# Three edits to the order of waits in a two-layer hybrid diffusion backbone: landing semaphores per row, later column sums, earlier query copies

## The reference

```python
for i in range(2):
    sh, sc, g = split(silu(c) @ ada_w[i] + ada_b[i], 3)      # modulation, for latent and for context
    u = rmsnorm(h, norm_g[i]) * (1 + sc) + sh
    if i == 0:   # window attention with a sink (8 heads) beside a Hyena long convolution (1024 wide)
        a, b = window_attention(q, k, v), hyena(u)            # q, k, v, hyena inputs, gate = u @ ev_w_in
        o = concat([a, b]) * silu(gate)
    else:        # grouped-query attention with rope (8 heads) beside latent attention (8 heads)
        o = concat([gqa(q, k, v), mla(q_up, kv_up)]) * silu(gate)   # latent tokens only
    h = h + g * (o @ w_out[i])
return h_lat
```

## Time and profile before

| | |
|---|---|
| three runs | 1456.12, 1457.83, 1458.51 us (median 1457.83) |
| profiled execution | 1455.26 us, span 1453.4 us, mean granted clock of TensorE 0.991 |
| busy share of the span | PE 97%, PEld (weight loads) 78%, DVE 72%, ACT 39%, POOL 24% |
| DMA | 273.28 MB, mean 188 GB/s |
| chain that ended last | PE 81%, DVE 9%, DMA 4%, ACT 2%, issue 2% |

### The profile page before, as it was taken

The page is one execution under the profiler, slowest core; times in us unless marked ns, Lnnn a source line. Parts: engine busy times, 40 slices in busy tenths (PEclk is TensorE's granted clock), DMA queues, the critical chain, the costliest instruction groups (busy, mean ns, idle before and its releaser), DMA issues.

```text
span 1453.4 us, 18246 instructions
## 1 busy us (share of the span) xinstructions
PE 1404.1 (97%) x7208; PEld 1134.6 (78%) x7208; DVE 1039.9 (72%) x1246; ACT 566.6 (39%) x826; POOL 354.5 (24%) x333
## 2 busy tenths in 40 slices
PE   5999999999999999998999899999999999999998
PEld 1336888888888878877888688888988878899887
DVE  3384999999999878887888545555645677677554
ACT  2554222222222344433433312214436666666432
POOL 1000543334433021201120133442100135432000
PEclk9999999999999999999999999999999999999999
DMA  9998555564555554445456866651424342323674
GB/s 348 406 371 330 175 174 200 159 208 157 201 162 166 189 180 148 151 154 192 140 185 231 300 204 221 220 189 63 159 87 151 139 145 91 114 94 110 224 239 145
DMA packets 63221, 273.28 MB, mean 188 GB/s; under 512 B 6736, under 2 KB 13088, under 8 KB 43296
## 3 DMA queue, kind: packets, MB, share of 16 engines
q1 hardware_dynamic: 42960, 194.51, 38.1%
q0 software_dynamic: 20176, 77.61, 16.7%
HBM read 257.40 MB, written 14.69 MB: 187 GB/s over the span
## 4 chain that ended last, share of the span: by engine, by line
PE 81%; DVE 9%; DMA 4%; ACT 2%; issue 2%; SPq 1%; POOL 0%; DVEq 0%; ACTq 0%
PE banks L1068 16%; PE banks L1069 16%; PE banks L1072 16%; DMA ada_ring<-in_ada_first 2%; PE banks L2268 2%; PE banks L2269 2%; PE banks L2274 2%; PE banks L1274 2%; DVE wl L1030 2%; PE banks L2025 2%; PE banks L2022 2%; PE banks L2019 2%; PE banks L2293 2%; PE banks L582 1%; DVE ada_acc L417 1%
## 5 line engine op out<-in xcount | busy, mean ns | idle before, releaser
L1068 PE MATMUL banks<-xh,wh 128*128 128x512 f32 (+1 forms) x1296 | 473.4, 373 | 0.0
L1069 PE MATMUL banks<-xl,wh 128*128 128x512 f32 (+1 forms) x1296 | 468.5, 369 | 0.0
L1030 DVE TENSOR_TENSOR wl<-raw,wh 128x2048 fp32r<-128x2048 f32 (+1 forms) x125 | 284.2, 2274 | 104.3 <-ACT wh L1024 104.3
L1024 ACT ACTIVATE wh<-raw 128x2048 fp32r<-128x2048 f32 (+1 forms) x125 | 236.7, 1894 | 241.0 <-PE banks L1072 126.5
L1068 PEld LDWEIGHTS banks<-xh,wh 128*128 128x128 f32 x1296 | 245.0, 189 | 46.4 <-issue 5.7
L1072 PE MATMUL banks<-xh,wl 128*128 128x512 f32 (+1 forms) x1296 | 279.8, 368 | 0.3 <-DVE wl L1030 0.3
L1069 PEld LDWEIGHTS banks<-xl,wh 128*128 128x128 f32 x1296 | 245.1, 189 | 40.3 <-issue 0.2
L1072 PEld LDWEIGHTS banks<-xh,wl 128*128 128x128 f32 x1296 | 227.1, 189 | 41.0 <-DVE wl L1030 0.5
L440 POOL DMA_DIRECT2D ada_w<-in_ada_rest x128 | 69.8, 545 | 486.4 <-DVE ada_acc L429 317.7
L417 DVE SCALAR_TENSOR_TENSOR ada_acc<-ada_w,cond,ada_acc 128x1024 f32<-128x1024 f32 x120 | 166.9, 1391 | 4.8 <-DMA ada_w<-in_ada_rest 2.8
L429 DVE SCALAR_TENSOR_TENSOR ada_acc<-ada_w,cond,ada_acc 128x1024 f32<-128x1024 f32 x90 | 131.4, 1460 | 0.0
(11 more groups left out here) (387 smaller groups left out, 2125.7 us busy)
## 6 DMA issues: line engine op xcount, KB each, us to landing
ada_w<-in_ada_rest POOLq DMA_DIRECT2D x128, 512.0 KB, 4.1
raw<-in_ev_tiles SPq DMA_DIRECT2D x52, 1024.0 KB, 6.5
ada_ring<-in_ada_first SPq DMA_DIRECT2D x32, 1024.0 KB, 12.9
raw<-in_out_tiles SPq DMA_DIRECT2D x16, 1024.0 KB, 6.2
raw<-in_od_wide SPq DMA_DIRECT2D x16, 1024.0 KB, 4.9
raw<-in_od_gates SPq DMA_DIRECT2D x16, 1024.0 KB, 5.0
raw<-in_out_wide SPq DMA_DIRECT2D x16, 1024.0 KB, 5.8
hT<-in_hT POOLq DMA_DIRECT2D x4, 1024.0 KB, 11.9
```

The costliest lines, as they stand in the source:

```text
L1024: nc.scalar.activation(b.wh[:, t % 2, 0:width], b.raw[:, t % 2, 0:width], ACT.Copy).then_inc(s.hi_done, 1)
L1030: nc.vector.tensor_tensor(b.wl[:, t % 2, 0:width], b.raw[:, t % 2, 0:width], b.wh[:, t % 2, 0:width].bitcast(F32), ALU.subtract).then_inc( ...
L1068: nc.tensor.matmul(out, wh[:, k, :], b.xh[:, seg, k, :], start=(k == 0), stop=False)
L1069: nc.tensor.matmul(out, wh[:, k, :], b.xl[:, seg, k, :], start=False, stop=False)
```

## The change

Three edits, independent of one another. First, `O_LAND` and `O_LANDED` go: rows whose buffer is one of the first seven use the semaphore of that buffer, the five rows of the other buffers (rows 6 to 10) use the five landing semaphores of the start's modulation ring (renamed `ring_landed`), counted on from there. A row waits for its own landing, or for the second landing in its buffer. With it the load of output tile 1's weights goes from between rows 11 and 12 to behind row 15. Second, the last three `ADA_SLOTS` are one higher, for TensorE's column sums and VectorE's store alike. Third, in layer 1 ScalarE copies the turned queries ahead of the slot's weight cut. The renaming in the start block is left out here.

```diff
-O_LAND = (0, 1, 2, 3, 4, 5, 6, 0, 1, 2, 3, 4, 0, 1, 2, 3)
-O_LANDED = (2, 2, 2, 2, 2, 1, 1, 2, 2, 2, 2, 2, 3, 3, 3, 3)
 O_ORDER = (0, 1, 2, 3, 4, 5, 6, 8, 9, 10, 11, 12, 13, 14, 7, 15)
 O_SLOT = (0, 1, 2, 3, 4, 5, 7, 8, 9, 10, 11, 6, 0, 1, 2, 3)
...
-ADA_SLOTS = (9, 17, 25, 33, 41, 49)
+ADA_SLOTS = (9, 17, 25, 34, 42, 50)
...
-                if i == 33:
+                if i == 34:
                     pe.wait_ge(s.rs_step, 2)
-                if i == 41:
+                if i == 42:
                     pe.wait_ge(s.rs_step, 5)
                 ada_columns(nc, pe, b, s, ps[7], n)
...
+def o_landed(s, n):
+    slot = O_SLOT[n]
+    if slot < ORING:
+        return s.out_o_in[slot], 16 * O_SLOT[:n + 1].count(slot)
+    i = slot - ORING
+    return s.ring_landed[i], 16 * (len(range(i, ADA_PIECES, ADA_RING)) + 1)
...
-    sp.dma_start(b.orow[O_SLOT[n]][:], g.o_d[k]).then_inc(s.out_o_in[O_LAND[n]], 16)
+    sp.dma_start(b.orow[O_SLOT[n]][:], g.o_d[k]).then_inc(o_landed(s, n)[0], 16)
...
-    act.wait_ge(s.out_o_in[O_LAND[n]], 16 * O_LANDED[n])
+    act.wait_ge(*o_landed(s, n))
...
         for n in range(11, KT):
-            if n == 12:
-                load_raw(sp, b, s, t0 + 1, out_weights(g, 1), (KT, P))
             load_o(sp, b, s, g, n)
+        load_raw(sp, b, s, t0 + 1, out_weights(g, 1), (KT, P))
...
         for i in range(4, L1_TILES):
             if i == FIRST_GATE:
                 token_drains(*DRAIN_SLOT[i])
+            if i - 1 in QUERY_TURN:
+                for r in range(2):
+                    keep_queries(QUERY_TURN[i - 1], r, 4 + r, 2 * (i - 20) + r + 1)
             split_high(nc, act, b, s, t0 + i + 1, l1_width(i + 1))
...
-            if i - 1 in QUERY_TURN:
-                for r in range(2):
-                    keep_queries(QUERY_TURN[i - 1], r, 4 + r, 2 * (i - 20) + r + 1)
```

More of the change, by code:

```diff
@@ L527, in _ @@
             sp.dma_start(b.ada_ring[p % ADA_RING], g.ada_first[p].rearrange("p (h k n) -> p h k n", h=2, k=2)).then_inc(
-                s.ada_pe_landed[p % ADA_RING], 16)
+                s.ring_landed[p % ADA_RING], 16)
             if p == 2:
@@ L577, in ada_matmuls @@
             grp, r = divmod(p, 4)
-            pe.wait_ge(s.ada_pe_landed[p % ADA_RING], 16 * (p // ADA_RING + 1))
+            pe.wait_ge(s.ring_landed[p % ADA_RING], 16 * (p // ADA_RING + 1))
             if r == 0 and grp > 0:
@@ L2889, in semaphores @@
     s.ada_lat = sem("ada_lat")
-    s.ada_pe_landed = [sem(f"ada_pe_landed{i}") for i in range(ADA_RING)]
+    s.ring_landed = [sem(f"ring_landed{i}") for i in range(ADA_RING)]
     s.ada_pe_used = sem("ada_pe_used")
```

## The result

The changed kernel takes 1446.51 us in the median of six runs (1444.86 to 1449.3), the kernel before 1458.83 in six runs beside them: a ratio of 0.9918, with a 95% interval from 0.9905 to 0.9931 (below, a ratio is given with its interval in brackets). The forecast was 1443.8, its range 1441 to 1449.

A forecast was written before the change was run, and what follows sets the result against it. TensorE was taken to bound the kernel, so only its waits and slowed stretches pay; -7.1 - 7.4 + 0.5 = -14.0 us, from a median of 1457.83 to 1443.8, range 1441 to 1449.

The forecast's parts named there:

- Part 1: Column sums one slot later: at slot 41, 4.8 us of wait and 2.3 of slow tile go; -7.1 us.
- rival (b): VectorE takes the column-sum gain back, TensorE waiting for low weights in slots 42 to 51: -6.9 us, 1450.9; chance 0.07.
- Part 2: Landing semaphore per row, output tile 1's weights behind row 15: output tile 1 starts at 821.3, not 828.69; -7.4 us.
- They do: In output tile 0, rows keep up with TensorE: they land 0.68 us apart, row 11 lands 2.7 us after issue.
- Rival (a): The clock drops in front of output tile 1 after 2.5 us idle, costing 2.3 us: -11.7, 1446.1; chance 0.2.
- Part 3: Layer 1, turned queries copied ahead of the weight cut: 2.2 us wait shrinks, later waits for weights appear; +0.5 us.
- Rival (c): Layer 1's query move keeps the 2.2 us it removes, VectorE's delay being absorbed: -16.7 us in all, 1441.1; chance 0.12.
- (d): Gated rows don't come earlier, another event holding ScalarE; the row change is worth -0.6: -7.2 us, 1450.6; chance 0.04.
- (e): Slower: output tile 1's weights starve, deciding point 17.8 us after issue; at 21 us, 3.2 slower, 1461.0; chance 0.03.

The follow-up runs named there:

- the hold: Changed kernel with GpSimd's first two 0.5 MB loads held until all 16 gated rows are cut; 1445.22 us, ratio 0.9914; again 1445.29 us, 0.9909.
- the second execution with both: Changed kernel, output tile 1's weights behind the eleven early rows, rope turns behind row 15, query copies in old place; second execution 1442.52 us, ratio 0.9893.

## Why the prediction came near, and where it was wrong

**Part 1** was right: -7.1 forecast, -7.12 in the trace, -7.4 in the run of its own. Tile 41 takes 7.36 us (655.62 to 662.98) at clock 1.00, so the 2.3 us of half clock came back together with the 4.8 us of waiting. No wait for low weights follows in slots 42 to 51; rival (b) is out.

**Part 2** was right in what it removes and wrong in one step: "They do", of rows that keep up, with row 11 landing 2.7 us and the weights 6.1 us after their issue. Both times came from a stretch in which GpSimd's loads were already through. The prediction never placed these two loads on the new scale. Counted from the first attention product behind tile 51, row 11's issue moved from +7.26 to +2.84, while the loads moved the other way, from +0.97 to +2.72, since GpSimd's work on the rope turns ahead of them took 6.56 us (795.21 to 801.77) instead of 4.74 (803.23 to 807.97); why it took longer is not shown. So they meet. Measured, 6.6 and 8.2 us: TensorE waits 1.42 for row 11 and output tile 1 starts at +16.60 instead of +14.3. With the loads held, row 11 lands in 3.2 and the start is +14.84 and +14.86. That the loads are the cause of most of this 2.3 us is shown by the hold; 0.5 us of it stays also there.

Of the two landings it is the weights' that sets the start: ScalarE is through with the rows at 811.80 and stands 1.89 us for the weights. But a time from issue to landing is the wrong kind of term for them, as the second execution of the changed kernel shows (SP's issue of the weights, ScalarE's copies from row 11 on and its cut of the weights):

```profile
811.65 0.51 SPq L1014 DMA_DIRECT2D raw<-in_out_tiles  x1
```

```profile
813.28 3.31 ACT L1841 ACTIVATE xh<-orow 128x512 fp32r<-128x512 f32 x5 [4.48 <-DMA orow<-gated]
...
818.47 1.91 ACT L1022 ACTIVATE wh<-raw 128x2048 fp32r<-128x2048 f32 x1 [1.88 <-DMA raw<-in_out_tiles]
```

There the weights were issued at +7.81 instead of +6.38, landed 6.8 us after issue instead of 8.2, and ScalarE cut them at the same +14.63. What came back is the moment at which row 11 is in (its copy starts at +9.44 both times) and the stretch behind it: four rows and 1 MB, 2.1 MB, in 5.2 us, about 400 GB/s with the DMA engines full. So in these two executions the bytes ahead of the weights set their landing, and not the moment of their issue.

The Trainium skill (DMA: Bandwidth & Descriptors, "Queues, rings and completion order") says that each DMA engine takes turns between the queues that have work, and drains a whole packet of descriptors from one before it goes to the next. This trace does not show such turns: in 804 to 805 GpSimd's queue moved 0.32 MB and SP's 0.01. The measurement decides; why SP's rows stood behind GpSimd's loads stays open. Row 11 was issued at +2.84 and landed at +9.4, with the hold at +3.16 and +6.3: 3.1 us later, somewhat more than the 2.7 us that the 1 MB of both loads takes at 393 GB/s.

**Rival (a)** came true beside it. The idle is 2.50 us, as forecast, though both of its ends are later, and the clock fell to a mean of 0.62 over the tile's first 4.5 us: 1.74 us, where the prediction put 2.3. It is the rest of part 2's miss: -7.4 forecast, +2.3 for landing, +1.7 for the clock, so -3.4. The chance of 0.2 was too low: of six executions with an idle of 2.2 to 2.6 us in front of output tile 1, one kept the clock. The prediction's own case for a kept clock, the 2.2 us wait in slot 20, did not hold every time either (see the end). Its case for rival (b), that VectorE runs without a gap up to 661, was misread, as it stood for 1.52 us at 653.18; nothing hung on it.

**Part 3** was right: +0.5 forecast, +0.37 and +0.38 measured, with the two new waits that the text named (0.8 for the high weights, 1.65 for the low ones) and the old one down to 0.36. The 0.63 us wait ahead of the first scores went, as said. Rival (c) is out, since the 2.2 us came back in these two. Rivals (d) and (e) are out: the rows came earlier, and the weights were there 8.2 us after issue, far from 17.8.

In sum the trace lost 4.0 us of forecast in part 2 and 0.63 in small pieces, and gained 0.83 in the start block. The median shrank by 12.3 us, more than the 10.3 of the two spans, for the profiled execution of before lay 3.6 us below the median of its runs, that of after only 1.65.

## What to carry to other kernels

A landing time holds only for the traffic it was read in, and with the DMA engines full the bytes ahead counted here, not the moment of issue: before a load is moved up, place every other queue's loads on the new scale as well, those of engines that the change doesn't touch too. A gap that is cut short in front of dense matmuls can still cost clock, so it pays to close it entirely (0.40 to 0.58 us left, full clock) rather than to half. And a wait taken from a tight engine's order returns as a wait for what was put behind it; count it in the next slot.

## What was not expected of the hardware

The granted clock did not follow the length of the idle alone. It fell after 2.23, 2.25, 2.46, 2.50 and 2.60 us in front of output tile 1, was kept once after 2.46, and fell in the middle of output tile 0 after 1.73. In slot 20, where part 3 is not in, it was kept in six executions after 2.15 to 2.19 us and fell in one after 2.20 (the second execution with both, 0.62 in 1158.0 to 1162.5). What decides was not found.

SP's issue of five rows took 3.49 and 4.61 us in two executions of the changed kernel, 2.87 and 3.21 with GpSimd's loads held, and 5.78, 4.47 and 3.14 behind 1 MB of weights on the same queue; the prediction reckoned with 1.88 for four. What sets it was not found.

The changed kernel reached the first attention product behind tile 51 at 799.05 in one execution and at 803.84 in another, with waits of 8.9 and 14.5 us for the start's modulation ring. These 4.8 us are more than most of the differences above, so they were read from that product on, and the time as a whole only with its interval.
